# First weights staged in later x blocks' space, row scalars on ScalarE, shift adds on VectorE, four square buffers in both first groups

## The reference, cut to what matters

```python
def modulate(h, shift, scale):
    return h * (1 + scale) + shift
...
    cc = jax.nn.silu(c)
        mod = (cc @ w_ada[l] + b_ada[l]).reshape(b, N_ADA, D_MODEL)
        sh1, sc1, gt1, sh2, sc2, gt2, sh3, sc3, gt3 = [mod[:, i, None, :] for i in range(N_ADA)]
        h = modulate(rms_norm(x, g_ffn1[l]), sh1, sc1)
        x = x + 0.5 * gt1 * swiglu(h, w_ffn1_in[l], w_ffn1_out[l])
        h = modulate(rms_norm(x, g_mix[l]), sh2, sc2)
        x = x + gt2 * token_mix(h, w_in[l], ...)
        h = modulate(rms_norm(x, g_ffn2[l]), sh3, sc3)
        x = x + 0.5 * gt3 * swiglu(h, w_ffn2_in[l], w_ffn2_out[l])
```

## Time and profile before

| what | value |
|---|---|
| time, median of 3 runs | 1633.8 us (1633.53 to 1641.79) |
| the profiled execution | 1635.23 us; the span of its slowest core, core 4, is 1633.7 us |
| spans of the 8 cores | 1622.2 to 1633.7 us |
| busy PE, DVE, ACT, POOL | 1515.0, 812.8, 487.1, 133.8 us |
| mean granted TensorE clock | 0.980 to 0.986 of full speed |

### The profile page before, as it was taken

One profiled execution on the slowest core, in us unless ns is written; L12 is line 12 of the kernel. 1 busy time (PEld: TensorE's weight loads), 2 busy tenths in 40 slices (PEclk: granted clock), 3 DMA queues, 4 the chain that ended last, 5 costly groups with the idle time before them and its releaser, 6 DMA issues.

```text
span 1633.7 us, 20428 instructions; the slowest of 8 cores (1622.2 to 1633.7 us)
## 1 busy us (share of the span) xinstructions
PE 1515.0 (93%) x6965; PEld 672.2 (41%) x7105; DVE 812.8 (50%) x1280; ACT 487.1 (30%) x624; POOL 133.8 (8%) x206
## 2 busy tenths in 40 slices
PE   2878999999999998988799987799989999999999
PEld 0323444444444443433344433344434444444444
DVE  3646637346346346656455456355336261624326
ACT  5552010110110115557743258543340101010110
POOL 0043000000010000000111000111030000001000
PEclk9989999999999999999999999799999999999999
DMA  9936252270370352030343420344203213105005
GB/s 278 302 95 128 53 127 54 62 151 14 90 149 13 90 138 44 1 53 0 52 76 66 69 48 1 52 78 78 52 6 73 52 27 59 26 14 84 13 1 206
DMA packets 47268, 121.61 MB, mean 74 GB/s; under 512 B 4288, under 2 KB 4416, under 8 KB 47040
## 3 DMA queue, kind: packets, MB, share of 16 engines
q0 software_dynamic: 30032, 57.81, 21.7%
q1 hardware_dynamic: 17136, 62.49, 12.0%
HBM read 169.70 MB, written 8.39 MB: 109 GB/s over the span
## 4 chain that ended last, share of the span: by engine, by line
PE 82%; DVE 5%; ACT 5%; issue 4%; DMA 2%; POOL 1%; DVEq 0%; SPq 0%; ACTq 0%; POOLq 0%
PE ps L179 82%; ACT arena L185 3%; DVE arena L194 2%; DVE arena L189 2%; POOL arena L201 1%; DVE arena L196 1%; DMA arena<-w_ap 1%; ACT arena L186 1%; DMA arena<-xT 1%; DMA arena<-w_ada 1%; ACT L186 0%; DVE arena L209 0%; ACT L185 0%; DVE arena L201 0%; DVE arena L212 0%
## 5 line engine op out<-in xcount | busy, mean ns | idle before, releaser
L179 PE MATMUL ps<-arena 128*128 128x512 bf16 (+5 forms) x6922 | 1503.8, 377 | 102.4 <-ACT arena L185 38.3
L179 PEld LDWEIGHTS ps<-arena 128*128 128x128 bf16 (+1 forms) x7060 | 667.5, 98 | 937.6 <-issue 188.8
L185 ACT ACTIVATE arena<-ps 128x512 bf16<-128x512 f32 (+4 forms) x368 | 270.4, 745 | 874.7 <-PE ps L179 826.3
L189 DVE TENSOR_TENSOR arena<-arena,ps 128x512 bf16<-128x512 bf16 (+1 forms) x230 | 175.1, 762 | 553.6 <-PE ps L179 489.5
L194 DVE SCALAR_TENSOR_TENSOR arena<-ps,arena 128x512 f32<-128x512 f32 (+1 forms) x410 | 315.5, 774 | 126.5 <-PE ps L179 72.1
L189 DVE TENSOR_TENSOR arena<-arena 128x512 bf16<-128x512 bf16 (+10 forms) x191 | 89.6, 495 | 44.5 <-ACT arena L185 36.0
L185 ACT ACTIVATE arena<-arena 128x1024 bf16<-128x1024 f32 (+2 forms) x114 | 102.5, 930 | 29.4 <-PE ps L179 16.0
L196 DVE SCALAR_TENSOR_TENSOR arena<-arena 128x1024 f32<-128x1024 f32 x72 | 87.8, 1220 | 13.1 <-DMA arena<-w_ada 10.4
L186 ACT ACTIVATE arena<-arena 128x512 bf16<-128x512 f32 (+1 forms) x84 | 57.8, 715 | 110.3 <-DVE arena L194 92.8
L194 DVE SCALAR_TENSOR_TENSOR arena<-arena 128x512 f32<-128x512 f32 (+2 forms) x114 | 79.7, 737 | 18.3 <-ACT arena L185 13.7
L201 POOL TENSOR_SCALAR arena<-arena 128x512 bf16<-128x512 f32 (+1 forms) x21 | 40.6, 1938 | 114.4 <-DVE arena L194 77.7
(11 more groups left out here) (17 smaller groups left out, 72.4 us busy)
## 6 DMA issues: line engine op xcount, KB each, us to landing
arena<-w_ada SPq DMA_DIRECT2D x72, 512.0 KB, 4.7
arena<-w_in POOLq DMA_DIRECT2D x28, 512.0 KB, 7.2
arena<-xT SPq DMA_DIRECT2D x20, 512.0 KB, 14.2
arena<-w3i POOLq DMA_DIRECT2D x20, 512.0 KB, 6.3
arena<-w1i POOLq DMA_DIRECT2D x16, 512.0 KB, 9.9
outT<-arena SPq DMA_DIRECT2D x16, 512.0 KB, 3.2
arena<-w1o POOLq DMA_DIRECT2D x10, 512.0 KB, 17.8
arena<-w3o POOLq DMA_DIRECT2D x10, 512.0 KB, 9.7
```

The source lines that it names most:

```text
L179: return self.op("pe", lambda e: e.matmul(out, lhsT=lhsT, rhs=rhs, start=start, stop=stop), reads=[lhsT, rhs], writes=[out])
L185: return self.op("act", lambda e: e.activation(out=out, in_=in_, func=func, scale=scale), r, [out])
L189: return self.op(eng, lambda e: e.tensor_tensor(out=out, in0=in0, in1=in1, op=op), [in0, in1], [out])
```

## The change

Nothing of what is computed changes, only where and when. (1) The eight `w1i` tiles no longer pass through the ring: they land in the memory of x blocks 3 and 4 (`XB[2]`, `XB[3]`), which are loaded later, and the ring serves the 16 `w_ada` tiles alone; 14 tiles are issued at once. (2) Scale and shift of the first norm are made by two small ScalarE instructions in place of two on VectorE; each sum, scale and shift has a cell of 64 bytes of its own (`RAW`), and two copies move them to `DER` at the end. (3) The shift adds of mode "pool" go to VectorE (mode "mix": even channel tiles on ScalarE, odd ones on VectorE). (4) Both first groups use four square buffers and four product buffers, and one rule places the norms: squares in two slots, statistics and half of the channel tiles in the next, the other half in the one after that; for a block whose first unit is `v`, slots `v-6` to `v-3`, and for block 2, which has no room, slots 4, 4, 5 and 6 (before: 4 to 7). For the later blocks the last piece moves from slot `v-2` to `v-3` in the first part, and from `v-1` to `v-3` in the second. (5) `ada_step` stands in other units. (6) The `EXPB` instructions are spread over the four groups after block 0's statistics. (7) `v_ones` goes from VectorE to GpSimd.

```diff
-                if mode == "act" or (mode != "dve" and kt % 2 == 0):
+                if mode == "act" or (mode == "mix" and kt % 2 == 0):
                     P.act(h[:, kt, :], t, AF.Identity, bias=DER[:, 3 * sub + 1, kt:kt + 1])
                 else:
-                    P.ts(h[:, kt, :], t, DER[:, 3 * sub + 1, kt:kt + 1], ALU.add, "pool" if mode == "pool" else "dve")
+                    P.ts(h[:, kt, :], t, DER[:, 3 * sub + 1, kt:kt + 1], ALU.add, "dve")
...
+    STAGE = [XB[2 + i // 4][:, 2 * (i % 4):2 * (i % 4) + 2, :].rearrange("p a b -> p (a b)") for i in range(8)]
+    slots = STAGE + [RING[i % 6] for i in range(16)]
...
-            P.load("sp", RING[n % 6], tiles[n], "d_a%d" % (n % 6))
+            P.load("sp", slots[n], tiles[n], "d_s%d" % n if n < 8 else "d_a%d" % ((n - 8) % 6))
...
-    for i in range(6):
+    for i in range(14):
         tile_load()
...
-            P.ts2(DER[:, 0, kt:kt + 1], MRAW[:, 8 + kt:9 + kt], B1[:, kt:kt + 1], CST[:, 80 + kt:81 + kt], ALU.add, ALU.mult)
-            P.tt(DER[:, 1, kt:kt + 1], MRAW[:, kt:kt + 1], CST[:, 8 + kt:9 + kt], ALU.add)
+            P.act(SCALE[kt], RAW[:, i - 1, 0:1], AF.Identity, scale=CST[:, 80 + kt:81 + kt], bias=B1[:, kt:kt + 1])
+            P.act(SHIFT[kt], RAW[:, i, 0:1], AF.Identity, bias=CST[:, 8 + kt:9 + kt])
...
+    P.copy(DER[:, 0, :], RAW[:, 16:24, 0])
+    P.copy(DER[:, 1, :], RAW[:, 24:32, 0])
...
+        for b in range(first, last + 1):
+            v = 4 * (bi + b - first)
+            st, ap = norm_parts(b, sub, "mix", sq4, tmp4)
+            for u, f in ((v - 6, st[:2]), (v - 5, st[2:4]), (v - 4, st[4:] + ap[:4]), (v - 3, ap[4:])):
+                if v == 4 * bi and u < lo + 2:
+                    u = lo if u < v - 4 else u + 1
+                slots.setdefault(u, []).extend(f)
...
+    N1 = norm_slots(2, 4, 0, 2, 4, o_w + 4 * 4096)
...
-        if bi >= 2 and u != 1:
+        if 4 * bi + u in (4, 7, 10, 11, 14, 15, 18, 19):
             ada_step()
...
-                    ng[2].extend([lambda h=h: P.act(EXPB[:, h, :], TABT[:, h, :], AF.Exp, bias=NB[:, h:h + 1])
-                                  for h in range(8)])
+                    for h in range(8):
+                        ng[3 + h // 2].append(lambda h=h: P.act(EXPB[:, h, :], TABT[:, h, :], AF.Exp, bias=NB[:, h:h + 1]))
...
-            P.memset(d, 1.0)
+            P.memset(d, 1.0, "pool")
             if b == 0:
-                P.ts(d, d, flag, ALU.mult)
+                P.ts(d, d, flag, ALU.mult, "pool")
...
-    N2 = norm_slots(3, 2, 2, 2)
+    N2 = norm_slots(3, 4, 2, 2, 0, base)
```

More of the change, by code:

```diff
@@ L479, in build_nc @@
     tiles = [w1i[half * NJ + j] for j in range(4) for half in (0, 1)]
-    tiles += [w_ada[8 * (1 - s_) + k] for k in range(8) for s_ in (0, 1)]
+    tiles += [w_ada[8 * s_ + k] for k in range(8) for s_ in (1, 0)]
+    STAGE = [XB[2 + i // 4][:, 2 * (i % 4):2 * (i % 4) + 2, :].rearrange("p a b -> p (a b)") for i in range(8)]
+    slots = STAGE + [RING[i % 6] for i in range(16)]
     tn = [0]
@@ L501, in build_nc @@
     B1 = view(o_b1, F32, (8,))
-    P.ts(B1, CST[:, 16:24], 1.0, ALU.add)
+    P.stt(B1, CST[:, 16:24], 1.0, CST[:, 80:88], ALU.add, ALU.mult)
+    RAW = view(base + 41984, F32, (32, 16))
+    SCALE = [RAW[:, 16 + kt, 0:1] for kt in range(8)]
+    SHIFT = [RAW[:, 24 + kt, 0:1] for kt in range(8)]
     def warm(n, bk, start, after=None):
@@ L517, in build_nc @@
             n = 2 * j + half
-            P.act(piece((0, 2)[j // 2] + half)[:, j % 2, :], RING[n % 6], AF.Copy)
-            tile_load()
+            P.act(piece((0, 2)[j // 2] + half)[:, j % 2, :], STAGE[n], AF.Copy)
     P.act(EPSC[:, 1:2], EPSC[:, 0:1], AF.Silu)
-    P.ts(EPSC[:, 2:3], EPSC[:, 0:1], EPSC[:, 0:1], ALU.add, "pool")
     for i in range(16):
-        slot = RING[(8 + i) % 6]
-        P.stt(slot, slot, 1.0, CB[:, :], ALU.mult, ALU.mult, accum=MRAW[:, 8 * (1 - i % 2) + i // 2:8 * (1 - i % 2) + i // 2 + 1])
+        slot = RING[i % 6]
+        P.stt(slot, slot, 1.0, CB[:, :], ALU.mult, ALU.mult, accum=RAW[:, i, 0:1])
         if i == 0:
@@ L529, in build_nc @@
             kt = i // 2
[L530 to L531 removed]
+            P.act(SCALE[kt], RAW[:, i - 1, 0:1], AF.Identity, scale=CST[:, 80 + kt:81 + kt], bias=B1[:, kt:kt + 1])
+            P.act(SHIFT[kt], RAW[:, i, 0:1], AF.Identity, bias=CST[:, 8 + kt:9 + kt])
             for b in range(2):
[L533 removed]
+                P.act(H[b][:, kt, :], XR[b][:, kt, :], AF.Identity, scale=SCALE[kt], bias=SHIFT[kt])
             for j in range(4):
@@ L655, in ffn, with norm_slots @@
         return pre, body
-    def norm_slots(first, nb, sub, start, lo=0):
+    def norm_slots(first, last, sub, bi, lo, scr):
         slots = {}
-        def put(v, *f):
-            slots.setdefault(v, []).extend(f)
-        free_at = lo
-        for q in range(nb):
-            v0 = max(4 * (start + q) - 7, free_at)
-            free_at = v0 + 2
-            v = [v0, v0 + 1, v0 + 2]
-            st, ap = norm_parts(first + q, sub, "pool")
-            put(v[0], st[0], st[1])
-            put(v[1], st[2], st[4], st[3], st[5])
-            put(v[2], st[6], st[7], st[8])
-            a0 = max(4 * (start + q) - 4, v[2])
-            n_ = 4 * (start + q) - a0
-            for i in range(8):
-                put(a0 + i * n_ // 8, ap[i])
+        sq4 = SQ + [view(scr + 2048 * i, BF16, (2, TB)) for i in range(2)]
+        tmp4 = TMP + [view(scr + 4096 + 2048 * i, F32, (TB,)) for i in range(2)]
+        for b in range(first, last + 1):
[5 more added lines that the diff above has]
+                slots.setdefault(u, []).extend(f)
         return slots
```

9 lines of the change are left out of this document (removed).

## The result

The changed kernel takes 1611.1 us (median of 4 runs, 1609.08 to 1691.62, three of them at most 1612.28), the kernel before 1633.7 (4 runs): a ratio of 0.985, 95% interval 0.981 to 0.989. Forecast were 1611 us, 1603 to 1619. In the 1691.62 run the four cores of one die had a granted clock of 0.94; the ratio leaves it out. The profiled execution took 1609.85 us, its slowest core (core 1) spans 1608.3.

The account below looks back on a forecast made before the run. PE, busy 93% of the span, was taken as the bound, so only its waits could be won. Terms 4.0 + 10.7 + 3.7 + 2.4 + 2.0 = 22.8 off 1635.2 gave 1612.4, less 1.4 for the median: 1611 us, range 1603 to 1619.

Parts of the forecast that it names:

- Staging and scalars: At the start, transfers would set the pace after the change, 1.57 us a tile: 4.0 us gained, bounds 0.9 and 8.1.
- the dip: At the start, transfers fell to 261 GB/s from 28 to 32 us; without it 0.9 us of transfers are won.
- The upper bound: At the start, at most 8.1 us gained (66.31 - 58.2), if VectorE's 1.3 us for each tile sets the pace.
- Adds and slots, first part: First part's first group: PE would lose 11.7 us instead of 22.4, so 10.7 gained; bounds 13.6 and 6.
- Second part: Second part's first group: 4.5 us lost instead of 8.2, so 3.7 gained; bounds 1.5 and 5.
- `EXPB` spread: Joint to the mixer: ScalarE's squares and PE come 2.4 us earlier, so 2.4 gained; bounds 0 and 4.3.
- `v_ones` to GpSimd: Before the attention: PE's wait of 2.01 us at 677.37 goes, so 2.0 us gained.
- Waits that stay in the first groups with a fall of the clock at each block: Rival: norms' chains hold PE at all blocks; first part gains 6, second 1.5, so 1618 us; chance 0.2.
- Quicker transfers without a fall of the clock: Rival: the start gains 6 to 8 us and block 2 another 2.9, so about 1605 us; chance 0.13.
- A change that does nothing much: Rival: start stays with the transfers, first groups' waits only move to VectorE's queue: 1627 to 1630 us; chance 0.05.
- GpSimd's fills hold VectorE: Rival: at the joint, four fills that read SBUF hold VectorE, 6.2 us lost, so 1617 us; chance 0.08.
- VectorE as the bound: Rival: VectorE bounds units 8 to 19; slower only above 26.2 us a block, ending above 1634 us; chance 0.02.

Follow-up runs that it names:

- the 0.8 of the same chip: Changed kernel with the first weights in the ring again: start 65.03 us, 1613.1 in all; against 64.25, undoing the staging costs 0.8 us.
- either edit alone: Changed kernel with odd channel tiles' shift adds back on GpSimd: 1623.5 us; or with the norms' slots as before and the adds on VectorE: 1621.4 us.
- the runs with block 2's edits: Changed kernel with filler matmuls in block 2's wait, or with all eight channel tiles of block 2 in one slot: first group 71.23 us in both.

## Why the prediction was right, step by step

*Staging and scalars*, 4.0 forecast, 4.2 measured. The first half of the mechanism holds: VectorE's pitch of 3.52 for a pair set the pace (the experiment with the scalars on VectorE). The second half, that the transfers set it after, holds only in part. The last product does wait for its transfer, at 1.58 a tile, but PE with its fillers takes 2.80 a channel tile, close to the 3.16 of two transfers, and the transfers cost PE no more than 0.8 to 1.6 us. The trace of before could have told this. That the forecast is so near is in part luck, because the two paces are so near. The 0.9 for the dip agrees with the 0.8 of the same chip; the 2.2 against the result's run is not excluded. The upper bound has a slip: 41.73 - 0.9 with twelve tiles at 1.3 and the 2.6 behind them is 59.0 and not 58.2, so 7.3 and not 8.1.

*Adds and slots, first part*, 10.7 forecast, 12.0 measured. On the profiled cores 62.1 us from 63.34 give 125.4; the last product starts at 136.10, so 10.7 are lost where 11.7 were forecast and 22.4 before. Block 2's waits are 3.01 + 1.10 = 4.1 (4.6 forecast); the clock costs 1.7 on core 1 and twice that on cores 2 and 3 (0.72 from 84 to 96 us), where 2.9 were forecast. Blocks 3 and 4 wait 0.94 and 0.40 + 0.35 + 0.95 = 1.7, where 1.4 and 1.5 + 1.3 were forecast; the 1.4 was not quite what the working gave, since 14.7 - 13.6 is 1.1. The forecast costed the two edits as one and kept the fall of the clock at blocks 3 and 4 for its lower bound. It did not say that either edit alone would leave such a fall, so that each alone is worth less than 4.

*Second part*, 3.7 forecast, 2.8 measured. The step that was off is the base: it took 8.2 us as lost from core 4, whose group took 65.23 us where the other seven had 63.60 or 63.61. On core 4 the group is 4.4 shorter than it was, 0.7 more than forecast; on the others 2.8.

*`EXPB` spread*, 2.4 forecast, 3.4 measured, inside its bounds. The waits were put too high (1.8 measured), and the fall of the clock behind them, which the working kept for the upper bound, was there before (0.86) and is gone: 1.6 more.

*`v_ones` to GpSimd*, 2.0 forecast, 0.8 measured. The wait went as forecast. What was missed is one wait later: behind the unchanged wait of 3.24 the clock fell on all eight cores of the profiled execution (10 matmuls in 3.60 to 4.00 us) and on none before. Cores on which it does not fall take 65.46 (three in each of the runs with block 2's edits), 2.2 under before.

*The sum.* The gains add up to 23.5 where 22.8 were forecast, which is closer than the terms are. Three came out higher by 0.2, 1.3 and 1.0 and two lower by 0.9 and 1.2; that they cancel is luck. The median of the runs has some luck too, since the slowest core is decided in a stretch that differs by 10 us from core to core.

*The rivals.* Waits that stay in the first groups with a fall of the clock at each block is what either edit alone does (1621 and 1623); the two together do not. Quicker transfers without a fall of the clock: 325 GB/s, and the clock falls at block 2; no. A change that does nothing much: 1611 is far from 1627. GpSimd's fills hold VectorE: its four multiplications with the flag at the joint took 0.93 us each, and PE's waits there are 0.35 to 1.38.

```profile
L201 POOL TENSOR_SCALAR arena<-arena 128x256 bf16<-128x256 bf16 x4 | 3.7, 926 | 0.7 <-POOL arena L212 0.7
```

The rule of the Trainium skill (SBUF — State Buffer, "SBUF: two separate sides") that such instructions take the ports by turns is not contradicted by this, but four of them at that size are too little to be seen in PE's waits. VectorE as the bound: from block 3's to block 4's first wait are 123.02 - 105.07 = 17.95 us, where 26.2 was the point from which it decided.

## What to carry to other kernels

Two edits that each shorten a wait can be worth little alone and much together, when only the short wait that both give is not followed by a fall of the granted clock; look at the clock behind each wait before costing one. A fall of the clock can also cost nothing, where the next wait takes up what it loses. Before a freed resource is named as the next bound, add up every engine's work per tile in that stretch, its fillers too. Hold a run against runs of the same chip: the unedited start differed by 1.4 us between chips, more than some of the effects read from it. And read a stretch on all cores: one core can carry a loss that the others don't have.
